# Activation buffers moved from 64 past a multiple of 128 bytes to a multiple of 128 bytes

## What is computed

```python
h = rmsnorm(x, attn_pre_g);  proj = h @ w_in            # 1024 -> 2328
o = concat(nsa_attention(...), swa_attention(...))      # 8 + 8 heads of 64
x = x + rmsnorm(o @ w_o, attn_post_g)
a, u = split(rmsnorm(x, mlp_pre_g) @ w_gate_up)         # 2 x 2816
x = x + rmsnorm((gelu(causal_dwconv(a)) * u) @ w_down, mlp_post_g)
x = x + (p @ w_ple) * sigmoid(x @ w_ple_gate)
# second block
q, k, v, rq, rk, rv, rg = split(rms_norm(x) @ w_in_2)
x = x + concat(neighbourhood_attention(q, k, v), silu(rg) * norm(retention(rq, rk, rv))) @ w_out_2
x = x + square(relu(rms_norm(x) @ w_up_2)) @ w_down_2   # 1024 -> 4096 -> 1024
return rms_norm(x)
```

## The kernel before

| what | address before | phase before | after | phase after |
|---|---|---|---|---|
| raw0 to raw4, wh0, wl0 to wh4, wl4, r_bc, r2_bc, sqr0, sqr1 | 16512 to 55423 | 0 | the same | 0 |
| small, ident, ones, cst | 55424, 55936, 56448, 56960 | 0 | the same | 0 |
| dn, ds (later nbi0, gd2) | 57984, 60032 | 0 | 57728, 59776 | 0 |
| tmp0, tmp2, tmp4 (2056 bytes each, rounded to 2112) | 61568, ... | 0 | 61312, ... | 0 |
| tmp1, tmp3 | 63680, ... | 64 | 63424, ... | 64 |
| AH, AL | 72128, 88512 | 64 | 71936, 88320 | 0 |
| BH, BL (and xin) | 104896, 121280 | 64 | 104704, 121088 | 0 |
| all behind them: q, k, v of both attentions, probabilities, X, ACC, PH, PL, tables | from 137664 | 64 | from 137472 | 0 |
| big1, big3, big5 (2056 bytes, rounded to 2112) | 180736, ... | 0 | 180544, ... | 64 |
| big0, big2, big4 | 178624, ... | 64 | 178432, ... | 0 |

## Time and profile before

### The profile page before, as it was taken

How to read it: one execution, slowest core, us unless ns; L and a number is a source line. 1 busy time by engine, 2 the same in 40 slices (tenths; PEclk the granted TensorE clock), 3 DMA queues, 4 the chain that set the end, 5 groups by cost and what they waited for, 6 DMA issues and landing times.

```text
span 1293.9 us, 16698 instructions
## 1 busy us (share of the span) xinstructions
PE 1278.1 (99%) x6136; PEld 1063.6 (82%) x6136; DVE 802.8 (62%) x1559; ACT 635.7 (49%) x1243; POOL 155.7 (12%) x146
## 2 busy tenths in 40 slices
PE   9999999999999999999999999999999999999998
PEld 8888888878888888888778777889888888888887
DVE  6699799685655565346788886578644343344334
ACT  6787576454335343234555655476543252342344
POOL 0022120000110011001002101022311030110111
PEclk9999999999999999999999999999999999999999
DMA  8211110433332333322323212432333323232321
GB/s 276 82 50 42 33 42 17 164 87 91 91 104 76 112 98 98 97 92 77 110 90 105 74 58 59 127 107 83 93 94 98 92 81 114 82 111 86 105 90 66
DMA packets 64624, 118.20 MB, mean 91 GB/s; under 512 B 7712, under 2 KB 12192, under 8 KB 64288
## 3 DMA queue, kind: packets, MB, share of 16 engines
q1 hardware_dynamic: 62704, 112.86, 28.7%
q10 hardware_dynamic: 1840, 4.29, 1.1%
HBM read 115.02 MB, written 2.10 MB: 91 GB/s over the span
## 4 chain that ended last, share of the span: by engine, by line
PE 87%; DVE 7%; issue 2%; ACT 2%; DMA 1%; POOL 0%; SPq 0%; POOLq 0%; DVEq 0%; ACTq 0%
PE bank L581 26%; PE bank L583 26%; PE bank L582 25%; PE bank L801 2%; PE bank L681 1%; PE bank L683 1%; PE bank L682 1%; DVE pp L2156 1%; PE bank L787 1%; PE bank L788 1%; DVE wl L1985 1%; DVE ptl L2178 1%; DVE pp L2173 1%; DMA raw<-in_w_swa 1%; DVE qs L2072 1%
## 5 line engine op out<-in xcount | busy, mean ns | idle before, releaser
L1985 DVE TENSOR_TENSOR wl<-raw,wh 128x512 fp32r<-128x512 f32 (+2 forms) x360 | 266.0, 750 | 326.6 <-ACT wh L1291 326.0
L1291 ACT ACTIVATE wh<-raw 128x512 fp32r<-128x512 f32 (+1 forms) x398 | 242.3, 619 | 287.6 <-PE bank L583 274.7
L581 PE MATMUL bank<-AH,wh 128*128 128x512 f32 (+1 forms) x848 | 333.0, 393 | 2.7 <-DVE AL L1999 0.8
L583 PE MATMUL bank<-AH,wl 128*128 128x512 f32 (+1 forms) x848 | 328.9, 388 | 0.0
L582 PE MATMUL bank<-AL,wh 128*128 128x512 f32 (+1 forms) x848 | 326.7, 385 | 0.0
L581 PE MATMUL bank<-BH,wh 128*128 128x512 f32 x624 | 248.4, 398 | 0.0
L583 PE MATMUL bank<-BH,wl 128*128 128x512 f32 x624 | 245.1, 393 | 0.0
L582 PE MATMUL bank<-BL,wh 128*128 128x512 f32 x624 | 243.8, 391 | 0.0
L581 PEld LDWEIGHTS bank<-AH,wh 128*128 128x128 f32 x848 | 159.5, 188 | 36.5 <-issue 4.0
L583 PEld LDWEIGHTS bank<-AH,wl 128*128 128x128 f32 x848 | 159.2, 188 | 35.3
L582 PEld LDWEIGHTS bank<-AL,wh 128*128 128x128 f32 x848 | 159.4, 188 | 33.0 <-issue 0.2
(11 more groups left out here) (336 smaller groups left out, 1632.0 us busy)
## 6 DMA issues: line engine op xcount, KB each, us to landing
raw<-in_w_dn SPq DMA_DIRECT2D x104, 256.0 KB, 2.6
raw<-in_w_gu SPq DMA_DIRECT2D x88, 256.0 KB, 2.6
raw<-in_w_up SPq DMA_DIRECT2D x64, 256.0 KB, 2.6
raw<-in_w_nsa SPq DMA_DIRECT2D x16, 256.0 KB, 2.6
raw<-in_w_pg SPq DMA_DIRECT2D x16, 256.0 KB, 2.7
raw<-in_w_naq SPq DMA_DIRECT2D x16, 256.0 KB, 2.6
nbi<-in_na_bias ACTq DMA_DIRECT2D x8, 448.0 KB, 3.3
raw<-in_w_swa SPq DMA_DIRECT2D x10, 256.0 KB, 3.0
```

The lines of the kernel that those rows point to most:

```text
L581: t.matmul(o, w, xh, start=start, stop=False, skip_group_check=skip)
L583: return t.matmul(o, wl, xh, start=False, stop=stop, skip_group_check=skip)
L1291: a.activation(W[i % NW].h[:, 0:n], RAW[i % NRAW][:, 0:n], ACT.Copy).then_inc(*s_wh.up(i))
L1985: v.tensor_tensor(w.l[:, 0:n], RAW[i % NRAW][:, 0:n], w.h[:, 0:n], ALU.subtract).then_inc(*s_wl.up(i))
```

## The change

The constant array `cst` is cut from 256 to 192 columns (256 bytes less; 177 columns are used), and 64 bytes are left out ahead of the region of A. What stood behind `cst` begins 256 bytes earlier up to the `tmp` buffers, and 192 bytes earlier from A on. Engines, instructions, their order, their waits, their sizes and their transfers are the same; only addresses differ, as the table above shows.

```diff
@@ -281,11 +281,12 @@
         small = new("small", 128)
         ident = new("ident", P)
         ones = new("ones", P)
-        cst = new("cst", 256)
+        cst = new("cst", 192)
         a_dn = region(896)
         dn = at("dn", 512, F32, a_dn)
         ds = at("ds", 256, F32, a_dn + 2048)
         a_tmp = [new(f"tmp{i}", T + 2) for i in range(5)]
+        top[0] += 64
         aA = region(8192)
         aB = region(8192)
         AH, AL = at("AH", 4096, F32R, aA), at("AL", 4096, F32R, aA + 16384)
@@ -383,7 +384,7 @@
         def cc(n):
             a = c_used[0]
             c_used[0] += n
-            assert c_used[0] <= 256
+            assert c_used[0] <= 192
             return cst[:, a:a + n]
```

## The result

| | before | after |
|---|---|---|
| median of the runs | 1295.26 us (1295.04 to 1295.59, 4 runs) | 1309.53 us (1307.36 to 1310.81, 4 runs) |
| span of the profiled execution | 1293.9 us | 1306.7 us |
| ratio, 95% interval | | 1.0112 (1.0099 to 1.0124), slower |

The change makes the kernel 1.1% slower, 14 us. The profiled execution after took 1308.47 us and accounts for 12.8 us of it in its span. The page after shows the same kernel otherwise: the same instructions, PE busy 99% as in the earlier trace rows, and a 9 for the granted clock in all slices.

The account below looks back on a forecast made before the run. PE was taken to bound the kernel, busy 99%, with 4320 matmuls each 15.5 ns over their columns, 67 us. All terms were put at 0, so the forecast was the time before, 1295.2 us, range 1283 to 1315.

Parts of the forecast that it names:

- What bounds the kernel: PE, busy 99% of the span: time is matmul count times pitch, with 15.5 ns surplus on 4320 matmuls, 67 us.
- DVE, ACT, weight loads, transfers: 0.: Outside PE's matmul pitch: small phase differences hidden by slack or inside the pitch, transfers unchanged; 0 us.
- The moving operand: 0.: All 4320 matmuls reading at phases (0, 0) instead of (64, 0): no effect, 0, with ends -8.8 and +4.5 ns each.
- The three neighbours: Streams at phases (0, 64), (64, 0) and (64, 64), with 233.3, 233.3 and 230 ns, taken to bound the moving operand's effect.
- equal phases bring no lower pitch: Four `sdl` by AH matmuls, both operands at phase 64: 230 ns each, so matching phases would not speed PE up.
- The argument against a lost 128-byte line: 256-column matmuls at phase 64: one extra line would make the lowest pitch 120 ns; the 113.3 ns seen excludes that.
- The rival "slower, the pitch of tokens": Streams of A and B go to 233.3 ns through moving phase 0: 4180 x 4.5 ns = 18.8 us, 1314 us; chance 0.26.
- The rival "faster": Same-phase moving and stationary reads lock better, surplus down to 6.7 ns: up to 38 us less, 1257 us; chance 0.24.
- the third of the full price: Partial gain in PE's pitch, about 12 us, 1283 us; chance 0.16 against 0.08 for all of it.
- The full one, 8.8 ns: Surplus of each of 4320 matmuls falls from 15.5 to 6.7 ns: 38 us, 1257 us; chance 0.08.
- The same, 1295.2: The forecast itself: the change does nothing to the whole kernel, 1295.2 us, own range 1292.5 to 1298; chance 0.50.

Follow-up runs that it names:

- cut_only: Kernel after the change without the 64 bytes ahead of A, so only the constants are cut; distance 64: 1294.22 us, ratio 1.0000.
- the map: Matmuls alone, all arrays at multiples of 512 bytes where an earlier such kernel had multiples of 128; distance varied by 32 bytes: 226.7 to 234.3 ns a matmul.
- a64_shift128: Kernel after the change with 128 instead of 64 bytes left out ahead of A, distance 192: 1309.79 us, ratio 1.0118.
- rel0: Kernel after the change with 192 instead of 64 bytes left out ahead of A, distance 0: 1285.16 us, ratio 0.9929.
- part (c): Stretches alternating between two phases in a kernel of matmuls alone: 231.8 and 231.7 ns with steps of 64, 228.3 and 230.0 with 128.

## Why the prediction was wrong

**What bounds the kernel** was read rightly, and so was the quantity: the surplus of 15.5 ns a matmul over its columns, 67 us in all, as the only term that addresses could move. The whole result lies in it. The measured 1309.5 us is inside the range of 1283 to 1315, but only because the range took in a rival; the forecast itself was no change.

**DVE, ACT, weight loads, transfers: 0.** Right. Their rows are unchanged to 2 ns in the kernel after the change, the chain still has 1% of DMA, and `cut_only`, with the `tmp` buffers moved, has a ratio of 1.0000.

**The moving operand: 0.** This is the step that failed: "nothing in the rows ties its value to a phase". The value is tied to a phase, but not to one of those that I tabulated. I wrote down addresses modulo 128 because the change speaks of 128, and saw (64, 0) with two pitches and (0, 64) with one. Modulo 256, and as a difference, the rows say more. `tokens` in the earlier trace rows has distance 192 and its 233.3 ns; the triple in the earlier trace rows has 64 and its 229; both are the map's values for these distances, shown by the same numbers in a kernel of matmuls alone and by the two forms changing places in `a64_shift128`. The change took the triples from distance 64 to 128, and the term that was put at 0 measured 3.5 ns on each of 4320 matmuls, 15 us. The addresses that it takes were in my own table.

**The three neighbours** were given too much weight. The six matmuls of the earlier trace rows at 233.3 ns do exist at distance 64: the rhythm can also settle on another value. But all such pieces end at the next interruption, after 12 or some 24 matmuls, and two of them have a neighbour that I should have looked at. At 712.48, and again at 830.62 (a piece that I had missed, so there are about 170 such matmuls and not 140), the triple follows `tokens` without a gap and goes on with the 233.3 ns of `tokens`, 24 matmuls in 5.60 us, until something else cuts it off. It need not: in `cut_only`, with the same distances, the first of these two pieces runs at 229.3. So at distance 64 a stretch can take either rhythm; that its beginning decides is not shown.

```profile
712.24 0.40 PE L683 MATMUL bank<-wl,BH 128*128 128x512 f32 x1
712.48 0.40 PE L581 MATMUL bank<-BH,wh 128*128 128x512 f32 x1
...
718.08 0.60 PE L702 MATMUL bank<-ident,r_bc 128*128 128x128 f32 x4
```

I let this minority stand as proof that phases don't matter; against it stood more than 4000 matmuls at 229 in the triple and all 192 of `tokens` at 233.3. The earlier trace rows has distance 0 and 230 ns, which I read as "equal phases bring no lower pitch"; the four matmuls there stand just behind a pause, and the map's stretches at distance 0 settle on 226.7 only after their start. Four matmuls were too few for that statement.

**The argument against a lost 128-byte line** (113.3 ns at 256 columns is below 120) was right, and stays so. But it excluded one mechanism and I took it for the exclusion of all.

**The rival "slower, the pitch of tokens"** is what happened, with the wrong address relation behind it: it named the moving operand's own phase 0, which `rel0` refutes (phase 0, faster than before) and `a64_shift128` too (phase 64, slow). Its price was 4.5 ns on 4180 matmuls, 18.8 us. Measured were 3.5 ns on all 4320, 15 us, since at distance 128 the triples keep 233.3 ns from 300 to 630 us only and have mostly 232.0 to 232.7 elsewhere. The medians show 14.3 us; the spans show 12.8, because the span before holds the 1.5 us of its fall of the clock.

**The rival "faster"** also exists, one step further: at distance 0 the triples have a mean of 227.0 ns, 2.1 less than before, and `tokens` has 6.4 less: 4320 x 2.1 + 192 x 6.4 = 10 us, of which the medians show 9. That is close to the third of the full price that I held for likelier than all of it. The full one, 8.8 ns, was nowhere seen with 512 columns: the 113.3 ns of the earlier trace rows stand at 256 columns (and at distance 64, where the map has 117.8; the other half of those rows has 117.8 too, by the starts in the trace), and 256 columns turned out not to tell of 512.

**The same, 1295.2** had the largest chance because I found no mechanism, and that is not what the chance should have rested on: the trace held three pitches and I could name the cause of none.

**What stays open** is why the distance acts. Shown is that the distance between the two operands is what counts at multiples of 32 bytes, that it has a period of 256 bytes, a sign, needs no other engine, and depends on the number of columns. That the reads of the moving operand and of the weights meet somewhere would fit, but which weights meet it, a matmul's own or the next one's, part (c) did not tell apart. Nor is it shown why one distance can settle on two rhythms, or what decides at 4, 8, 24 and 252 bytes.

## What to carry to other kernels

Where PE is busy all through, measure its pitch (start to start) and compare it with the columns divided by the clock; the surplus of 13 to 21 ns at 512 float32r columns here depended, at multiples of 32 bytes, on the address of the moving operand minus that of the stationary one, modulo 256 bytes. Place weight and activation arrays so that this difference is 0 (both at multiples of 256, with slices and chunks at multiples of 256 as well); rounding both to 64 or 128 leaves it to chance, and a buffer that grows by 64 bytes far ahead in the layout can cost 1%. For matmuls of 256 columns the best of the four distances tried was another, 192, so try a few offsets rather than trust the rule. And when two profiles are compared to a microsecond or two, look at the clock in short windows first: a fall of 3.4 us is not seen in the page's slices.

## What the runs showed of the hardware

- The pitch of matmuls of 512 columns in float32r, each with a weight load of its own, at a granted clock of 1.00 (2.4 GHz, 213.3 ns for the columns): 226.7 ns at distance 0, 228.8 at 64, 232.2 at 128, 234.3 at 160; 237.8 at 4 bytes, where the moving operand is also off a multiple of 16.
- The Trainium skill, "TensorE: Matmul & The Clock Gate", section "Step-by-step: what each phase is for", has two independent SBUF read ports for the moving operand and the weights, so that loading the next weights takes no read bandwidth from the running matmul. The traces agree that loads run beside matmuls (188 ns inside a pitch of 229). But the same matmuls with the same loads have 226.7 ns at distance 0 and 234.3 at 160, so the relation of the two addresses is not without effect; whether the two reads hinder each other is not shown.
- One distance can have two rhythms: at 64, 24 triples ran at 233.3 ns behind `tokens` (712.48 to 718.08 of before) and the same ones at 229.3 in `cut_only`; at 128, the long stretch at 300 us had 233.3 and the one at 940 us 232.4.
- The granted clock fell from 1.00 to 0.5 (1.2 GHz) for 3.4 us in the profile of before, and 512 columns took 426 ns a matmul there instead of 229.
- The rhythm has inner structure: three pitches that repeat (232, 226, 229) at distance 64, an alternation of 229 and 238 at 300 us after the change, a group of seven at 1100 us. A mean over a triple or two is no measure of it; the first start to start after a pause was 333 to 342 ns at 512 columns in the maps.
